# Value projection of the prompt attention: four heads at once in every second head group, products of 256 columns instead of 128

## What is computed

```
def _mla_attend_prompt(q_nope, q_pe, c_kv, k_pe, w_uk, w_uv):
    ...
    k_nope = jnp.einsum("bkr,rhd->bkhd", c_kv, w_uk)
    v = jnp.einsum("bkr,rhd->bkhd", c_kv, w_uv)
    ...
        p = jax.nn.softmax(sc, axis=-1).astype(v.dtype)
        return jnp.einsum("bhqk,bkhd->bqhd", p, v)
```

## Time and profile before

| | |
|---|---|
| median of three executions | 1641.25 us |
| the profiled execution | 1638.68 us |
| its span, first to last instruction | 1636.8 us |
| TensorE busy | 1474.2 us, 90% of the span |
| TensorE weight loads busy | 1365.1 us, 83% |
| VectorE, ScalarE, GpSimd busy | 871.0, 528.0, 586.5 us |
| mean granted clock of TensorE | 0.951 of full speed |
| moved by DMA | 160.51 MB, 98 GB/s |

### The profile page before, as it was taken

How to read it: one execution, slowest core, us unless ns; L and a number is a source line. 1 busy time by engine, 2 the same in 40 slices (tenths; PEclk the granted TensorE clock), 3 DMA queues, 4 the chain that set the end, 5 groups by cost and what they waited for, 6 DMA issues and landing times.

```text
span 1636.8 us, 29300 instructions
## 1 busy us (share of the span) xinstructions
PE 1474.2 (90%) x11936; PEld 1365.1 (83%) x11936; DVE 871.0 (53%) x1735; ACT 528.0 (32%) x1026; POOL 586.5 (36%) x748
## 2 busy tenths in 40 slices
PE   4989999999999999999976889999957999999995
PEld 4989788898988889888864668789957999999994
DVE  5574687877878777786874322213344222222225
ACT  3232343424344343434423222222223333222221
POOL 1443252342524334142310222234443444444451
PEclk9888999999999999999987889999977999999997
DMA  3223222222223222222220698733311232222221
GB/s 118 65 69 94 83 79 78 83 76 82 73 77 88 80 78 74 84 85 65 83 90 4 186 292 267 240 113 117 104 39 52 94 97 83 95 98 91 91 91 65
DMA packets 109590, 160.51 MB, mean 98 GB/s; under 512 B 16497, under 2 KB 83569, under 8 KB 109457
## 3 DMA queue, kind: packets, MB, share of 16 engines
q1 hardware_dynamic: 56592, 130.14, 24.9%
q10 hardware_dynamic: 52864, 28.51, 6.0%
HBM read 145.87 MB, written 12.74 MB: 97 GB/s over the span
## 4 chain that ended last, share of the span: by engine, by line
PE 62%; DVE 25%; issue 4%; ACT 4%; ACTq 2%; SPq 1%; POOL 1%; DMA 1%; DVEq 0%; POOLq 0%
PE lin L456 51%; PE Pb L589 2%; DVE arena L1313 2%; PE lin L645 2%; ACTq L1061 2%; DVE arena L1312 2%; DVE arena L1314 1%; DVE arena L1311 1%; DVE sm L1384 1%; PE Pb L487 1%; PE lin L495 1%; DVE arena L1419 1%; ACT arena L970 1%; DVE arena L1319 1%; PE Pb L748 1%
## 5 line engine op out<-in xcount | busy, mean ns | idle before, releaser
L413 POOL TENSOR_TENSOR w_lo<-w_stage,w_hi 128x256 fp32r<-128x256 f32 x736 | 574.4, 812 | 1002.9 <-ACT w_hi L849 1002.9
L456 PE MATMUL lin<-act_hi,w_hi 128*128 128x260 f32 x1760 | 371.2, 293 | 19.7 <-DVE acc L1580 8.6
L456 PE MATMUL lin<-act_lo,w_hi 128*128 128x260 f32 x1760 | 360.4, 287 | 0.0
L456 PEld LDWEIGHTS lin<-act_hi,w_hi 128*128 128x128 f32 x1760 | 277.6, 194 | 29.4 <-issue 22.0
L456 PEld LDWEIGHTS lin<-act_lo,w_hi 128*128 128x128 f32 x1760 | 278.6, 194 | 0.0
L849 ACT ACTIVATE w_hi<-w_stage 128x1024 fp32r<-128x1024 f32 x184 | 193.7, 1053 | 247.1 <-PE lin L456 229.3
L456 PE MATMUL lin<-act_hi,w_lo 128*128 128x260 f32 x1760 | 234.6, 286 | 0.0
L456 PE MATMUL lin<-mid_hi,w_hi 128*128 128x260 f32 x1024 | 211.3, 288 | 14.3 <-DVEq L1499 6.2
L456 PEld LDWEIGHTS lin<-act_hi,w_lo 128*128 128x128 f32 x1760 | 220.8, 190 | 3.3 <-issue 3.3
L456 PE MATMUL lin<-mid_lo,w_hi 128*128 128x260 f32 x1024 | 207.7, 285 | 0.0
L456 PEld LDWEIGHTS lin<-mid_hi,w_hi 128*128 128x128 f32 x1024 | 159.7, 191 | 21.1 <-issue 12.7
(11 more groups left out here) (238 smaller groups left out, 1906.8 us busy)
## 6 DMA issues: line engine op xcount, KB each, us to landing
w_stage<-in_wall SPq DMA_DIRECT2D x184, 512.0 KB, 3.7
arena<-in_cache SPq DMA_DIRECT2D x124, 144.0 KB, 3.2
arena<-in_state ACTq DMA_DIRECT2D x16, 512.0 KB, 5.3
out_stateT<-arena ACTq DMA_DIRECT2D x16, 512.0 KB, 4.0
o_attn<-in_cache SPq DMA_DIRECT2D x64, 128.0 KB, 3.6
o_attn<-in_cache ACTq DMA_DIRECT2D x64, 128.0 KB, 3.9
arena<-in_xT SPq DMA_DIRECT2D x8, 520.0 KB, 5.8
out_yT<-arena SPq DMA_DIRECT2D x8, 260.0 KB, 2.1
```

The source lines that it names most:

```text
L413: low = pool.tensor_tensor(w_lo[:, slot, part], w_stage[:, slot, part], w_hi[:, slot, part].bitcast(F32), ALU.subtract)
L456: mm = pe.matmul(lin[:, pl.slot, hf, 0:HALF], w[:, ch.slot, off:off + P], r[:, hf * HALF:(hf + 1) * HALF], start=(k == 0 and p == 0), stop ...
```

## The change

In groups 0, 2, 4 and 6 the block `uv` holds the values of four heads: the group's own two and the two of the next group. The products have 256 columns instead of 128, their number stays 24, the result fills both banks of the slot, and the two copies into `V` (twice as wide now) have 512 columns each instead of 256. In groups 1, 3, 5 and 7 the block `uv` doesn't exist: no products, no copies, no place in the sequence of `lin`. The weights of the four heads lie in the chunk UKV of the even group; that chunk of an odd group keeps its size and has zeros there. The attention of group g reads its half of `V` by `128 * (g % 2)`.

```
+ODD_LIN = [name for name in STEADY_LIN if name != "uv"]
+C_LIN = [FIRST_LIN] + [ODD_LIN if i % 2 else STEADY_LIN for i in range(1, 8)] + [LAST_LIN]
...
-        V = part(512, "p (c v) -> p c v", c=NCH)
+        V = part(1024, "p (c v) -> p c v", c=NCH)
...
-                            wh = w_hi[:, ch.slot, 512 + k * P:640 + k * P]
-                            wl = w_lo[:, ch.slot, 512 + k * P:640 + k * P]
+                            wh = w_hi[:, ch.slot, 512 + 256 * k:768 + 256 * k]
+                            wl = w_lo[:, ch.slot, 512 + 256 * k:768 + 256 * k]
                             for n, (x, w) in enumerate(((a, wh), (a, wl), (b, wh))):
-                                mm = pe.matmul(lin[:, pl.slot, 0, c * P:(c + 1) * P], x, w,
+                                mm = pe.matmul(lin[:, pl.slot, c // 2, 256 * (c % 2):256 * (c % 2) + 256], x, w,
...
-                        mm = pe.matmul(Pb[64 * h:64 * h + 64, pb, 0:P], V[:, j, 64 * h:64 * h + 64],
+                        mm = pe.matmul(Pb[64 * h:64 * h + 64, pb, 0:P],
+                                       V[:, j, 128 * (g % 2) + 64 * h:128 * (g % 2) + 64 * h + 64],
...
-                pe.wait_ge(S["lin_free"], c_lin(i - 1, "uv").index + 1)
+                pe.wait_ge(S["lin_free"], c_lin(i - 1, "uk" if g % 2 else "uv").index + 1)
...
-                    value_rows()
+                    if i % 2 == 0:
+                        value_rows()
                     latent_queries()
...
+                    if i % 2:
+                        return
                     pl = c_lin(i, "uv")
                     done(pl)
-                    act.activation(V[:, 0:2, :], lin[:, pl.slot, 0, 0:256].rearrange("p (c v) -> p c v", c=2), ACT.Copy
+                    act.activation(V[:, 0:2, :], lin[:, pl.slot, 0, :].rearrange("p (c v) -> p c v", c=2), ACT.Copy
...
+                    if i % 2:
+                        return
                     pl = c_lin(i, "uv")
                     done(pl)
-                    dve.wait_ge(S["v_act"], i + 1)
-                    dve.tensor_copy(V[:, 2:4, :], lin[:, pl.slot, 0, 256:512].rearrange("p (c v) -> p c v", c=2)
+                    dve.wait_ge(S["v_act"], i // 2 + 1)
+                    dve.tensor_copy(V[:, 2:4, :], lin[:, pl.slot, 1, :].rearrange("p (c v) -> p c v", c=2)
```

More of the change, by code:

```diff
@@ L62 @@
 LIN_C = len(PRE_LIN)
-LIN_D = LIN_C + len(FIRST_LIN) + 7 * len(STEADY_LIN) + len(LAST_LIN)
+LIN_D = LIN_C + sum(len(order) for order in C_LIN)
 LIN_OV = LIN_D + NB * len(ROW_LIN)
@@ L109, in c_lin @@
 def c_lin(i, name):
-    return c_place(LIN_C, FIRST_LIN, STEADY_LIN, LAST_LIN, i, name)
+    return fixed(LIN_C + sum(len(order) for order in C_LIN[:i]) + C_LIN[i].index(name))
 def c_chunk(i, name):
@@ L140 @@
 SMALL = {}
-ARENA = 18836
+ARENA = 19348
 DMA_SCRATCH = 1024
@@ L1739, in group_rest @@
             uk = w_uk[:, 2 * g:2 * g + 2, :].reshape(KV_LORA, P)
-            uv = w_uv[:, 2 * g:2 * g + 2, :].reshape(KV_LORA, P)
-            put(tiles(uk), uk.T, tiles(uv))
+            if g % 2:
+                put(tiles(uk), uk.T)
+            else:
+                put(tiles(uk), uk.T, tiles(w_uv[:, 2 * g:2 * g + 4, :].reshape(KV_LORA, 2 * P)))
         else:
```

## The result

The changed kernel took 1647.88 us in the median of ten executions (1646.2 to 1652.29), the kernel before, run beside it, 1641.48 us (1638.44 to 1647.7). The ratio is 1.0036, with a 95% interval of 1.0021 to 1.0050: 3.4 to 8.2 us slower. The forecast was 1643.4 us in a range of 1640.0 to 1647.2, so the time fell just above the range. The profiled execution took 1650.27 us, 11.6 us more than that of before.

A forecast was written before the change was run, and what follows sets the result against it. The prediction took the copies releasing s0, not TensorE's own work, to bound the group ends. Even groups +2.7 us and odd groups -0.6 us summed to +2.1 us, 1643.4 us on the median, range 1640.0 to 1647.2.

The forecast's parts named there:

- What bounds the place: End of a group: s0 is released by the copies, VectorE's last, and not by TensorE's own work.
- Even groups: Groups 0, 2, 4, 6: longer products and two serial copies add 0.67 us before the next block, +2.7 us over four.
- Odd groups with a full clock: Groups 1, 3, 5, 7: s0 could start 0.9 us sooner, but waiting for GpSimd leaves 0.14 us each, -0.6 over four.
- the forecast's rule: GpSimd and VectorE on SBUF: each waits until the other has ended; the one that waited longer goes first.
- rival A: Odd groups: the clock falls in the new pause, 0.5 to 1.2 us per fall, about 1647 us; chance 0.28.
- The forecast (with none or one fall of the clock): Whole kernel: +2.1 us, 1643.4 us, or +2.6 to +3.3 us if the clock falls once; chance 0.47.
- The second argument: Against clock falls: the clock stayed full through groups 1 and 2, whose shorter pauses add up to some 5 us.
- The price of a fall: Odd groups: 1.2 us lost at half clock, up to 0.7 absorbed by the GpSimd wait, so 0.5 to 1.2 us.
- B: Odd groups: GpSimd's fourth part runs directly behind its third, giving -3.0 us, sum -0.3, 1641.0 us; chance 0.15.
- C: Odd groups: the saved products' time arrives, up to 2.5 us each, sum -7.3, 1634.0 us; chance 0.07.
- D: Even groups: the copies don't count, since something else holds s0 by 0.6 us anyway; 1641.0 us, chance 0.03.

The follow-up runs named there:

- the filled version: The change with 18 idle products of 256 columns, results unused, put behind `ql` in groups 1, 3, 5 and 7: 1642.76 us, ratio 0.9994.
- the odd part alone: Kernel before with `uv` left out of odd groups, even groups keeping 24 products of 128 columns and narrow copies: 1650.83 us, ratio 1.0033.
- the even part alone: The change in even groups only; odd groups keep their 24 products of 128 columns and narrow copies: 1644.61 us, ratio 1.0001.
- the two versions made from before: Kernel before with `latents_out()` ahead of `silu(3)`, which waits for GpSimd's split: 1643.1 us; the same plus side-by-side copies of `V`: 1641.81 us; both ratio 1.0000.
- The last experiment: Kernel before with 7 idle products of 256 columns between `queries(1)` and `keys()` of groups 1 to 7: 1641.18 us, ratio 0.9996.
- the best version: The change plus 18 idle products, `latents_out()` ahead, `silu(3)` waiting for GpSimd's split, copies of `V` side by side: 1638.83 us (0.9959), again 1638.53 us (0.9976).
- the kernel before with order and copies: Kernel before with `latents_out()` ahead of `silu(3)`, which waits for GpSimd's split, and both copies of `V` side by side: 1641.81 us, ratio 1.0000.

## Why the prediction was wrong

**What bounds the place: right.** s0 was released by VectorE's copies. The pause was forecast at 2.35 us and was 2.14.

**Even groups: right.** Forecast +0.67 us each; 97.87 to 97.97 us after 97.25 is +0.6 to +0.7, group 0 +0.54. Term by term, at the end of group 2 (two products of `uv`, the two copies, s0):

```profile
330.88 0.28 PE L553 MATMUL lin<-w_hi,mid_hi 128*128 128x256 f32 x1
331.01 0.28 PE L553 MATMUL lin<-w_lo,mid_hi 128*128 128x256 f32 x1
...
331.44 0.60 ACT L951 ACTIVATE arena<-lin 128x512 f32<-128x512 f32 x1 [2.10 <-PE lin L553]
...
332.14 0.69 DVE L1355 COPY arena<-lin 128x512 f32<-128x512 f32 x1 [0.89 <-PE lin L564]
...
332.93 0.48 PE L458 MATMUL lin<-mid_hi,w_hi 128*128 128x260 f32 x2 [0.80 <-issue]
```

Products 0.12 us apart, ScalarE's copy 0.60 us (forecast 0.595), VectorE's 0.69 (0.688), one behind the other, and s0 right behind.

**Odd groups with a full clock: right in mechanism, 0.2 us off.** Forecast -0.14 us each; with the filled pause they take 97.33 to 97.45 after 97.25, so +0.1. It was the third of GpSimd's parts that had to wait for `silu(3)`, not the fourth:

```profile
231.78 1.42 POOL L415 TENSOR_TENSOR w_lo<-w_stage,w_hi 128x256 fp32r<-128x256 f32 x1
...
233.16 0.72 POOL L415 TENSOR_TENSOR w_lo<-w_stage,w_hi 128x256 fp32r<-128x256 f32 x1
```

(GpSimd's third and fourth part of SA, end of group 1 after the change: 1.42 and 0.72 us.) `silu(3)`, issued at 231.89, got its turn at once and lasted 0.71 us, although the third part's record begins 0.11 us ahead of it. So the forecast's rule, that the one that waited longer goes first, isn't what happened here. The low weights were ready at 233.88, within 0.1 us of where I had them relative to `ql`. The missing 0.2 us can be read in group 1 of the filled version. Counted from the group's `bB`, `ql` started at 81.47 us, where `uv` had started at 81.31 before, so s0's low-weight products came at 86.31, no sooner than before (86.30); and the four of them took 0.74 us behind their wait in place of 0.65.

**The step that failed** is the weight of rival A, "Against it: here the idle part is only 2.35 us", and with it the likeliest case, "The forecast (with none or one fall of the clock)". I compared the pause with two longer ones (3.0 and 2.8 us) and took the difference as safety. But the same trace of before holds a pause of the forecast's very length, 2.37 us, and a fall behind it (a product of TensorE, then windows as above):

```profile
1096.29 0.25 PE L786 MATMUL lin<-olat_hi,w_hi 128*128 128x16 f32 x1 [2.37 <-issue]
...
1096.00:1098.00 2.00, 1.71 (x11) 1.74 (x11) 0.19 (x1) 1.06 (x1) 0.23 (x1) 0.69 0.00 0
1098.00:1100.00 2.00, 2.00 (x11) 2.00 (x11) 0.00 (x0) 0.00 (x0) 2.00 (x4) 0.50 0.00 0
```

The clock fell at 1096.8, and another time at 888.5, 0.5 us behind a pause of 1.95 us. The second argument, the full clock through groups 1 and 2, was no safety either: at ends of groups with the products of before it fell 8 times in 28. After the change it fell in 12 of 12 odd groups without `uv` and without filling (the change twice, the odd part alone), in none of 20 with 18 idle products, in 1 of 4 with 9. The 24 products had been what kept TensorE at work there. So the term of the odd groups, forecast at -0.6 us with the clock put at nothing, was +5.1: +0.4 by the chain of waits and +4.7 by the clock.

**The price of a fall was undersized.** Forecast 0.5 to 1.2 us. Against the same groups of the filled version the falls in the first profile cost 1.9 us in group 1 (6.8 us of half clock), 0.7, 1.4 and 0.7 in groups 3, 5 and 7 (3.4 us each), 4.7 us together; in groups that wait for nothing else at the s blocks one costs 1.5 us (97.3 to 98.8). I had counted on the wait for GpSimd to absorb part of each fall; the falls show that only where the half clock begins before it: those that began within 0.3 us of the start of s0 cost 0.6 to 0.7 us, those some 2 us behind it 1.4 to 1.5.

**The sum.** In the first profile: even groups and group 0 +2.5, odd groups +0.4 and falls +4.7, 7.7 us within 0.1. Rival A, as written, "about 1647", was the right case with a chance of 0.28, and its upper end, 1648.2, contains the result; the range was cut at 1647.2, inside this case. B, C and D didn't happen.

**What stays open.** The two profiled executions differ by a further 3.9 us outside the group ends. Behind the last `bB` the untouched code took 807.3 us before and 812.8 after, with the clock at half for 131 us before and for 147 after; the profiles of all runs here, with the same code in it, lie between 806.0 and 812.8. So the clock is a part of it, but what makes it fall more often in one execution isn't shown. Nor is it settled why the filled version isn't 2 us slower than before. Falls at unchanged ends of groups (8 of 28 in the profiles of before, of the odd and the even part alone, and of the two versions made from before) at some 1.5 us each would add 3 us to a typical execution of the kernel before (an estimate: 8/28 of 7 ends, times 1.5), and would fit. The last experiment, which should have lowered the median by that, is too coarse to show it or to exclude it. It would also mean that the best version gains by its clock, of which no run is a test.

## What to carry to other kernels

Taking work from an engine is worth what the next step gains at that place: find who releases the step behind, before counting instructions saved. Where TensorE waits anyway, removing its products makes a pause, and here the pause had a price of its own, paid by the products behind it at half the clock. Watch the granted clock, and look in the trace of before for every pause of that length, not only for the longest; if the work can't be put to use, idle products can fill the pause, which cost nothing here. Wait chains move: after freeing one slot, look at which slot the very next block takes. And when several edits together give a gain, run them without the change: here they brought a group as far alone.

## What the runs showed of the hardware

- The granted clock fell at 12 of 12 pauses of 2.1 us, from 0.5 us ahead of their end to 2.2 us behind it, once in four with a pause of 1.0 us, and at 8 of 28 ends of unchanged groups, whose pauses are up to 0.9 us between full blocks; it came back after 3.4 or 6.8 us. The same code lost its clock in one execution and kept it in another, and falls can come in several groups in a row (groups 2, 3 and 4 of one profile). At the 27 ends of groups 2, 4 and 6 with products of 256 columns in `uv` it never fell, which no run was made to explain. The Trainium skill, page TensorE: Matmul & The Clock Gate, section "What's actually happening", ties the clock to how busy the engine has been. The runs agree: with 18 products of 256 columns and unused results in the pause the clock stayed full at 20 of 20.
- GpSimd's parts and VectorE's instructions with two SBUF operands took turns. At the ends of the odd groups after the change `silu(3)` kept its 0.71 us and the GpSimd part behind another one grew from 0.72 to 1.42, although its record begins 0.11 us sooner; in group 1 of the kernel before with order and copies a part that began 0.09 us ahead of VectorE kept 0.74 us, and VectorE's instruction took 1.20 in place of 0.70.
- Products of 16, 128 and 256 columns with a new stationary operand each started 0.11, 0.111 and 0.12 us apart at a full clock, so a product of 256 columns costs nearly the same as one of 128.
